# Layer 0's front in another order, with all 16 shifted copies of each channel tile issued from GpSimd

## The chip, the cores and the metric

One core of a Trainium2 chip runs the whole program. TensorE (PE) multiplies, VectorE (DVE), ScalarE (ACT) and GpSimd (POOL) do the rest, and DMA queues move data; SyncE (SP) only issues DMAs. The metric is the device time of one execution in microseconds, lower is better.

## The reference

Two decoder layers run over 512 prompt rows and 8 x 8 sample rows. Only layer 0's mixer matters here:

```
z = rmsnorm(x, norm1[0]) @ conv_w_in                # 1024 -> 2*768 + 256
u = z[:, :768] * sigmoid(z[:, 768:1536])            # GLU
y = causal depthwise conv of u, width 31, 768 channels, + bias
mix = silu(layernorm(y))                            # over the 768 channels
qm = z[:, 1536:]                                    # queries into 256 memory tokens, 4 heads
km, vm = rmsnorm(mem) @ w_mem_kv[0]                 # for the prompt; cached for the samples
x = x + concat(mix, attend(qm, km, vm)) @ w_out     # then a SwiGLU FFN; layer 1 follows
```

## The kernel before

**Weights.** All big products run on an exact split of float32: a chunk of weights is loaded by SP into one of two `raw` buffers, ACT rounds it to `wH` (`hi`, L1111), DVE makes the rest `wL` (`lo`, L446), and PE adds three products (`product`, L1626). SP's loads (`conv_load`, L2255) wait until the buffer's last chunk has been split (`lo_done`). Whatever else SP issues stands in the same queue.

**Front (0 to 46 us).** ACT's queue loads x (`xin`), POOL's loads the memory tokens (`mem`, L2406), and SP's loads the small vectors (`vrow`), the taps `dwrow`, two weight chunks and the conv history (`crow`). PE transposes x and the vectors; it waits for `vec_in`, which counts `dwrow` too. ACT squares x in five pieces (L1272) with `hi(0)` between the second and the third, so that the last three squares wait for the first weight chunk. The row sums go back through PE (L1797) as a broadcast, and `norm(0)` (L466, L1129, L470) makes the activations in eight steps that pace the first product. `lo(1)` follows the norm.

**Taps.** Each of six channel tiles (c = 0 to 5) is convolved by PE and DVE. PE takes `PE_GROUPS[c]` groups of four taps (L1815, L1818): it multiplies `Q`, four copies of `gated` shifted by 0 to 3 columns, with diagonal matrices `diag`. `shifted(c)` makes `Q` by 16 DMAs of 32 partitions (L2276, SP's queue); it waits for `gated` of tile c (`u_done`) and for PE's last use of `Q` (`taps_ready`), since there is one `Q`. `diagonals(c)` (POOL, L2431) needs `dwq`, 16 small DMAs of `dwp` (L2311, SP). DVE adds the taps that are left, 15 of 31 for tiles 0 to 3, none for 4 and 5 (`taps`, L737 and L741).

**Order.** PE's order is written by hand: products 0 and 1 (queries), conv tile 0 (two products), four memory chunks (L1714, the key-value product), conv tile 1, then for c = 2 to 5 conv tile c and `taps(c-1)`, with one prompt unit or sample group of the memory attention between matmul steps. Sample keys (`ks`) are transposed in conv tile 1 (`group_keys`, L1856); POOL loads them with the sample values `vs` when the last memory chunk has been used. At the end PE sums tiles 0 to 3 over channels (`sums`, L1936), runs `taps(5)` with the second sample group between its steps, and sums tiles 4 and 5.

**LayerNorm.** DVE subtracts the mean (L853), ACT squares (L1398) into two buffers of `sq`, DVE adds the six squares one after another (L860), and PE sums the result once. ACT copies `usc` (conv state of the samples, L1392) ahead of the squares. Then come the square root (L1400), DVE's reciprocal (L863), ACT's copies of the new conv states (L1407, L1409), Silu (L1412) and the split of the result, and the output projection at 276 us.

Of the kernel before, what the change touches and what calls it, by code (L numbers as in the profile page):

```python
# [39 lines left out]
def build(nc, x_prompt, x_sample, cache_conv, cache_fox_k, cache_fox_v, cache_fox_logf,  # L40
# [38 lines left out]
    PE_GROUPS = [4] * (KC - 2) + [NQT] * 2  # L79
# [37 lines left out]
    VEC_LOADS, LATE_LOADS = 6 + 8 + 1, 2 + 1  # L117
# [35 lines left out]
    with ExitStack() as ctx:  # L153
# [93 lines left out]
        Q, o = at("Q", [P, 4, UL], o)  # L247
        diag, o = at("diag", [P, 2, 4, NQT, DQ], o)
# [13 lines left out]
        dg = sq[:].rearrange("p a n -> p (a n)")[:, 0:(TT + 1) * P].rearrange("p (t q) -> p t q", q=P)  # L262

# [72 lines left out]
        vec_in, hist_in, mem_in, pages_in = (sem(n) for n in ("vec_in", "hist_in", "mem_in", "pages_in"))  # L336
# [96 lines left out]
        def _(dve):  # L433
# [271 lines left out]
            last.then_inc(dg_done, 1)  # L705

# [143 lines left out]
            squares = tmp[:, 0]  # L850
            for c in range(KC + 1):
                if c < KC:
                    nc.vector.tensor_tensor(yc[:, c], yc[:, c], rb[:], ALU.subtract).then_inc(lny_done, 1)  # L853
                if c == 1:
                    dve.wait_ge(ysq_done, 1)
                    nc.vector.tensor_copy(squares, sq[:, 0]).then_inc(ysq_used, 1)
                elif c:
                    dve.wait_ge(ysq_done, c)
                    dve.wait_ge(ysq_used, c - 1)
                    nc.vector.tensor_tensor(squares, squares, sq[:, (c - 1) % 2], ALU.add).then_inc(ysq_used, 1)  # L860
# [242 lines left out]
        def _(act):  # L1103
# [175 lines left out]
            norm(0)  # L1279
# [60 lines left out]
            hi(1)  # L1340
# [38 lines left out]
            y_begin(KC - 2)  # L1379
            for b in range(GS):  # L1380
                group_keys(1, b)
# [9 lines left out]
            for c in range(KC):  # L1391
                last = nc.scalar.activation(usc[:, c], sample_rows(c)[:, :, NQ:NQ + H], ACT.Copy)  # L1392
            last.then_inc(usc_done, 1)
            for c in range(KC):
                act.wait_ge(lny_done, c + 1)
                if c >= 2:
                    act.wait_ge(ysq_used, c - 1)
                nc.scalar.activation(sq[:, c % 2], yc[:, c], ACT.Square).then_inc(ysq_done, 1)  # L1398
# [192 lines left out]
        def _(pe):  # L1591
# [201 lines left out]
            transposes([dwrow[:, c * P:(c + 1) * P] for c in range(KC)])  # L1793
# [4 lines left out]
            mm.then_inc(ss_ready, 1)  # L1798

# [5 lines left out]
            def taps(c, beside=None):  # L1805

                pe.wait_ge(q_in, 16 * 4 * TAPS * (c + 1))
                pe.wait_ge(diag_ready, c + 1)
                n = PE_GROUPS[c]
                for q in range(n):  # L1810
# [3 lines left out]
                    for a in range(4):  # L1814
                        nc.tensor.matmul(ps[DQ * a:DQ * a + DQ, 4, 0:SEQ], diag[0:k, c % 2, a, q, :], Q[0:k, a, TAPS * q:TAPS * q + SEQ],  # L1815
                                         start=(q == 0), stop=(q == n - 1), skip_group_check=True, tile_position=(0, DQ * a))
                    for a in range(4):
                        mm = nc.tensor.matmul(ps[DQ * a:DQ * a + DQ, 5, 0:NS].rearrange("p (b n) -> p b n", b=NB), diag[0:k, c % 2, a, q, :],  # L1818
                                              Q[0:k, a, H + SEQ:UL].rearrange("p (b n) -> p b n", b=NB)[:, :, TAPS * q:TAPS * q + NQ],
# [114 lines left out]
            def sums(src, c, first, last, bank):  # L1934
                for h in range(2):
                    mm = nc.tensor.matmul(ps[:, bank + h, 0:HT], ones[:], src[:, h * HT:(h + 1) * HT], start=first, stop=last)  # L1936
                if last:
                    mm.then_inc(ln_ready, 1)
            history(0)
            history(1)  # L1940
            product(0, 0, 0, aH, aL, 0, KD, True, True, (a_ready, 0))
            product(1, 0, 1, aH, aL, 0, KD, True, True, beside=lambda k: head_sums(0) if k == 5 else None)
# [24 lines left out]
            for c in range(KC - 2, KC):  # L1967
                pe.wait_ge(y_begun, c + 1)
                sums(yc[:, c], c, False, c == KC - 1, 0)
            group_out(1)  # L1970
            pe.wait_ge(ysq_used, KC)
            sums(tmp[:, 0], 0, True, True, 4)
# [275 lines left out]
        def _(sp):  # L2248
# [20 lines left out]
            def shifted(c):  # L2269

                sp.wait_ge(u_done, c + 1)
                if c:
                    sp.wait_ge(taps_ready, c)
                for g in range(TAPS):
                    for a in range(4):
                        sp.dma_start(Q[DQ * g:DQ * g + DQ, a, 0:UL - g], gated[DQ * a:DQ * a + DQ, c, g:UL]).then_inc(q_in, 16)  # L2276

# [21 lines left out]
            sp.dma_start(dwrow[:], conv_dw[0]).then_inc(vec_in, 16)  # L2299
            assert loads + 1 == VEC_LOADS  # L2300
            conv_load(0)
            conv_load(1)
            for G in range(GR):
# [4 lines left out]
            sp.wait_ge(dwp_done, 1)  # L2308
            for g in range(TAPS):
                for a in range(4):  # L2310
                    sp.dma_start(dwq[DQ * g:DQ * g + DQ, a], dwp[DQ * a:DQ * a + DQ, g]).then_inc(dwq_in, 16)  # L2311
            for n in range(2, C_WO0 + 4):
                if n == C_MEM0 + 3:
                    shifted(0)
                for c in range(1, KC):
                    if n == MP + N_MEM + 2 * (c + 2) + 1:
                        shifted(c)
# [61 lines left out]
        def _(pool):  # L2379
# [28 lines left out]
            def sample_loads(l, G):  # L2408

                mb = MBS[l]  # L2410
                for name, cache, semaphore in (("ks", cache_mem_k, ks_in), ("vs", cache_mem_v, vs_in)):
                    if G and name == "ks":
                        if l:
                            pool.wait_ge(tr_free, marks["ksT", l, G - 1])
                        else:
                            pool.wait_ge(sk_in, GS * G)
                    elif G:
                        pool.wait_ge(at_pv, (2 * len(MEM_UNITS) + GR if l else 0) + G)
                    pool.dma_start(mb[name][:].rearrange("p b t n -> p (b t) n"),
                                   cache[l, G * GS:(G + 1) * GS].rearrange("b (t p) h d -> p (b t) (h d)", p=P)).then_inc(semaphore, 16)  # L2420
# [6 lines left out]
            def diagonals(c):  # L2427

                if c >= 2:
                    pool.wait_ge(taps_ready, c - 1)  # L2430
                nc.gpsimd.tensor_tensor(diag[:, c % 2], dwq[:, :, c, :].unsqueeze(3).broadcast_to([P, 4, NQT, DQ]),  # L2431
                                        m32[:].unsqueeze(1).unsqueeze(1).broadcast_to([P, 4, NQT, DQ]), ALU.mult).then_inc(diag_ready, 1)
            memory(0)
            one = lambda instruction: step(instruction, which=1)
            one(nc.gpsimd.memset(m32[:], 0.0))
            for a in range(4):
                one(nc.gpsimd.affine_select(out=m32[:], in_=m32[:], compare_op=ALU.not_equal, fill=1.0, base=-DQ * a, pattern=[[-1, DQ]],
                                            channel_multiplier=1))
            pool.wait_ge(dwq_in, 16 * 4 * TAPS)
# [73 lines left out]
            sample_loads(1, 0)  # L2513
            sample_loads(1, 1)
# [57 lines left out]
```

## Time and profile before

| | us |
|---|---|
| median of 3 runs | 1941.47 (1938.92 to 1941.77) |
| the profiled execution | 1936.35 |
| its span, first to last instruction | 1934.7 |
| PE busy in the span | 1706.0 (88%) |
| layer 0's mixer in the span, up to the output projection | 276 |
| POOL busy in the span | 114.3 (6%) |

The profiled execution is 5.1 us under the median of the runs; 1.65 us of it lie outside the span. Times in the text are from the span's start. The granted TensorE clock is given in parts of full speed: 1.00 is 2.4 GHz and 0.50 is 1.2 GHz.

### The profile page before, as it was taken

To read this page: it belongs to the slowest core of one execution; us is meant where nothing else is said; L and a number is where in the kernel's file an instruction comes from. 1 tells how busy PE (TensorE), PEld (TensorE's weight loads), DVE (VectorE), ACT (ScalarE), POOL (GpSimd) and SP (SyncE) were. 2 spreads that over 40 slices of the span, in tenths; PEclk is the share of its full clock that TensorE was granted. 3 is DMA by queue.
4 is the path that set the end of the run, shared out by engine and by line. 5 is a ranking of instruction groups with operands and counts; after the bars stand their busy time and mean duration, and the time that the engine had idled before them with its cause. 6 is when DMAs were issued, how large, how long until landed. Compare 5 with 4: busy or idle time off the path is not lost.

```text
span 1934.7 us, 37856 instructions
## 1 busy us (share of the span) xinstructions
PE 1706.0 (88%) x15345; PEld 1494.4 (77%) x15345; DVE 865.3 (45%) x1209; ACT 588.7 (30%) x1050; POOL 114.3 (6%) x220
## 2 busy tenths in 40 slices
PE   4889868999999998999867777788779899999999
PEld 3767567999999997899644444444449899999998
DVE  5657365333323223675466555555414533333121
ACT  4344253322222112433322333333322322222121
POOL 1011000000000001444100000000000000000000
PEclk7899979999999999999886788888869899999999
DMA  4464311222223232233425677777662222223331
GB/s 125 124 176 117 94 51 54 85 79 79 84 87 93 76 89 69 61 81 83 157 93 187 220 253 256 259 258 262 199 205 77 66 82 81 87 82 93 103 88 55
DMA packets 245588, 235.37 MB, mean 122 GB/s; under 512 B 14594, under 2 KB 202644, under 8 KB 245466
## 3 DMA queue, kind: packets, MB, share of 16 engines
q1 hardware_dynamic: 235914, 212.54, 35.7%
q0 software_dynamic: 8896, 18.79, 3.3%
q10 hardware_dynamic: 656, 2.36, 0.3%
q8 instruction: 83, 1.36, 0.3%
q14 instruction: 39, 0.32, 0.1%
HBM read 215.37 MB, written 7.80 MB: 115 GB/s over the span
## 4 chain that ended last, share of the span: by engine, by line
PE 76%; DVE 9%; DMA 5%; SPq 3%; issue 3%; ACT 3%; POOL 0%; DVEq 0%; ACTq 0%; POOLq 0%
PE ps L1626 57%; DMA vring<-in_cache_fox_v_dram 4%; PE ps L2149 4%; PE ps L2194 2%; PE ps L1815 2%; DVE tmp L466 1%; PE ps L2128 1%; SPq L2345 1%; DVE aL L470 1%; PE ps L1605 1%; PE ps L1714 1%; PE ps L1695 1%; DVE yc L737 1%; PE ps L2154 1%; DMA raw<-in_conv_w_in_dram 1%
## 5 line engine op out<-in xcount | busy, mean ns | idle before, releaser
L1626 PE MATMUL ps<-aH,wH 128*128 128x288 f32 x2224 | 490.1, 302 | 41.1 <-DVE aL L470 32.1
L1626 PE MATMUL ps<-aH,wL 128*128 128x288 f32 x2224 | 478.4, 297 | 0.0
L1626 PE MATMUL ps<-aL,wH 128*128 128x288 f32 x2224 | 478.1, 297 | 0.0
L1626 PEld LDWEIGHTS ps<-aH,wH 128*128 128x128 f32 x2224 | 360.5, 191 | 55.2 <-issue 32.4
L446 DVE TENSOR_TENSOR wL<-raw,wH 128x1024 fp32r<-128x1024 f32 (+1 forms) x179 | 232.0, 1296 | 301.8 <-ACT wH L1111 299.4
L1626 PEld LDWEIGHTS ps<-aL,wH 128*128 128x128 f32 x2224 | 361.4, 191 | 0.0
L1626 PEld LDWEIGHTS ps<-aH,wL 128*128 128x128 f32 x2224 | 361.3, 191 | 0.0
L1111 ACT ACTIVATE wH<-raw 128x1024 fp32r<-128x1024 f32 (+1 forms) x179 | 198.8, 1111 | 364.8 <-PE ps L1626 323.2
L1626 PE MATMUL ps<-gH,wH 128*128 128x288 f32 x704 | 151.6, 296 | 0.0
L1626 PE MATMUL ps<-gH,wL 128*128 128x288 f32 x704 | 151.0, 295 | 0.0
L1626 PE MATMUL ps<-gL,wH 128*128 128x288 f32 x704 | 150.9, 295 | 0.0
L2194 PE MATMUL ps<-vring,pTs 128*32 128x256 f32 x768 | 93.2, 485 | 58.7 <-DMA vring<-in_cache_fox_v_dram 57.4
L660 DVE TENSOR_TENSOR tmp<-ps,sq 128x576 f32<-128x576 f32 x44 | 33.3, 758 | 178.3 <-PE ps L1626 178.3
L1626 PEld LDWEIGHTS ps<-gL,wH 128*128 128x128 f32 x704 | 112.8, 188 | 0.0
L1626 PEld LDWEIGHTS ps<-gH,wH 128*128 128x128 f32 x704 | 112.7, 188 | 0.0
L1626 PEld LDWEIGHTS ps<-gH,wL 128*128 128x128 f32 x704 | 112.7, 188 | 0.0
L992 DVE STREAM_TRANSPOSE kset<-kset 128x1536 f32<-128x1536 f32 x64 | 109.5, 1751 | 0.0
L2194 PEld LDWEIGHTS ps<-vring,pTs 128*32 128x32 f32 x768 | 27.2, 125 | 103.2 <-DMA vring<-in_cache_fox_v_dram 80.2
L1250 ACT ACTIVATE gH<-tmp 128x576 f32 (+1 forms) x44 | 30.2, 686 | 246.2 <-DVE tmp L660 246.2
L636 DVE TENSOR_TENSOR xT<-xT,ps 128x576 f32<-128x576 f32 (+1 forms) x32 | 24.1, 754 | 150.5 <-PE ps L1626 150.5
L2149 PE MATMUL ps<-kset,qx 32*32 32x256 f32 x3072 | 76.3, 414 | 4.9 <-issue 4.8
L2149 PEld LDWEIGHTS ps<-kset,qx 32*32 32x32 f32 x3072 | 58.6, 109 | 19.4 <-issue 12.2
(352 smaller groups left out, 1670.3 us busy)
## 6 DMA issues: line engine op xcount, KB each, us to landing
kset<-in_cache_fox_k_dram SPq DMA_DIRECT2D x128, 384.0 KB, 4.0
vring<-in_cache_fox_v_dram SPq DMA_DIRECT2D x128, 384.0 KB, 4.8
raw<-in_w_gate_up_dram SPq DMA_DIRECT2D x88, 512.0 KB, 3.8
raw<-in_w_down_dram SPq DMA_DIRECT2D x32, 704.0 KB, 4.5
raw<-in_fox_w_in_dram SPq DMA_DIRECT2D x21, 512.0 KB, 4.0
raw<-in_w_out_dram SPq DMA_DIRECT2D x16, 512.0 KB, 3.7
raw<-in_conv_w_in_dram SPq DMA_DIRECT2D x14, 512.0 KB, 4.5
raw<-in_w_mem_kv_dram SPq DMA_DIRECT2D x8, 512.0 KB, 3.5
```

Source lines behind the costliest of these rows:

```text
L446: nc.vector.tensor_tensor(wL[s][:, 0:size], raw[:, s, 0:size], wH[s][:, 0:size].bitcast(F32), ALU.subtract).then_inc(lo_done, 1)
L466: nc.vector.scalar_tensor_tensor(out=tmp[:, k % 2], in0=xT[:, k], scalar=vec[:, gain + k:gain + k + 1], in1=rb[:], op0=ALU.mult, op1=ALU.m ...
L470: nc.vector.tensor_tensor(aL[:, k - 1], tmp[:, (k - 1) % 2], aH[:, k - 1].bitcast(F32), ALU.subtract).then_inc(a_ready, 1)
L636: nc.vector.tensor_tensor(x, x, acc(j0 % 2), ALU.add).then_inc(x_new, 1)
L660: nc.vector.tensor_tensor(halves(tmp[:, f0 % 2]), acc(2 * (f0 % 2) + 1), halves(sq[:, f0 % 2]), ALU.mult).then_inc(g_done, 1)
L992: nc.vector.transpose(where, where).then_inc(kt_done, 1)
L1111: nc.scalar.activation(wH[s][:, 0:size], raw[:, s, 0:size], ACT.Copy).then_inc(hi_done, 1)
L1250: nc.scalar.activation(gH[:, f, :].rearrange("p o n -> p (o n)"), tmp[:, f0 % 2], ACT.Copy).then_inc(gH_done, 1)
L1626: mm = nc.tensor.matmul(ps[:, 2 * slot + h, 0:HT], weights[:, w], a[:, k0 + k, h * HT:(h + 1) * HT], start=(first and x == 0 and weights i ...
L1815: nc.tensor.matmul(ps[DQ * a:DQ * a + DQ, 4, 0:SEQ], diag[0:k, c % 2, a, q, :], Q[0:k, a, TAPS * q:TAPS * q + SEQ], start=(q == 0), stop=( ...
L2149: nc.tensor.matmul(out(a, j).rearrange("p (g i) -> p g i", g=SPG), qx4[r, blk, :], kset[x][r, :, blk * DQ:blk * DQ + DQ], start=(m == 0 an ...
L2194: mm = nc.tensor.matmul(ps[QR * j:QR * j + QR, 4, 0:4 * DH], pTs[:, k, QR * j:QR * j + QR], vring[n % VRING][:, 4 * DH * j:4 * DH * (j + 1 ...
```

## The change

- **Front.** `dwrow` gets its own semaphore and is loaded after the two weight chunks. POOL loads `mem` after all of x. ACT runs all squares of x first, then `hi(0)`, `hi(1)`, `norm(0)`, and only then the squares of `mem`. DVE runs `lo(0)`, `lo(1)`, `norm(0)`, and only then the tap rows (`dwp`) and the history. PE transposes `dwrow` after the broadcast of the row sums, and the second half of the history in product 1.
- **Queues.** The 16 DMAs of `dwq` and the 96 of `Q` go from SP's queue to POOL's. `ks` is loaded as soon as `mem` has been read, `vs` at its old place.
- **Last tile.** Tile 5 has its own buffer `Qlast` (over the activations `aH`, which are free by then), so its copies don't wait for `taps(4)`. Tile 4 gets 4 groups on PE and 15 taps on DVE, which stand around the second sample group's softmax steps.
- **LayerNorm.** The squares go to four buffers; PE sums tiles 0 to 3 itself, DVE adds only the last two. `usc` is copied earlier, and a Silu of one column behind the square root brings Silu's table load forward.

```diff
-    PE_GROUPS = [4] * (KC - 2) + [NQT] * 2
+    PE_GROUPS = [4] * (KC - 1) + [NQT]
...
+        Qlast, e_ = at("Qlast", [P, 4, UL], aH_at)
+        def square_of(c):
+            return (sq, tmp)[c // 2 % 2][:, c % 2]
+        def copies(c):
+            return Qlast if c == KC - 1 else Q
...
             lo(0)
+            lo(1)
             norm(0)
-            lo(1)
+            tap_rows()
+            history(0)
+            lo(2)
             memory_rows(0)
-            history(0)
             history(1)
-            lo(2)
...
+            taps(KC - 2, 0)
             group_top(1)
+            taps(KC - 2, 1)
             group_scale(1)
+            taps(KC - 2, 2)
...
-            for c in range(KC + 1):
-                if c < KC:
-                    nc.vector.tensor_tensor(yc[:, c], yc[:, c], rb[:], ALU.subtract).then_inc(lny_done, 1)
...
+            for c in range(KC):
+                nc.vector.tensor_tensor(yc[:, c], yc[:, c], rb[:], ALU.subtract).then_inc(lny_done, 1)
+            dve.wait_ge(ysq_done, KC)
+            nc.vector.tensor_tensor(square_of(KC - 1), square_of(KC - 1), square_of(KC - 2), ALU.add).then_inc(ysq_used, 1)
...
-                if t == 1:
-                    hi(0)
...
+            hi(0)
+            hi(1)
+            norm(0)
             memory_rows(0)
-            norm(0)
...
+            nc.scalar.activation(stat[:, 63:64], eps[:, 0:1], ACT.Silu)
...
+            for c in range(KC - 2):
+                pe.wait_ge(ysq_done, c + 1)
+                sums(square_of(c), c, c == 0, False, 4, ysq_summed)
+            pe.wait_ge(ysq_used, 1)
+            sums(square_of(KC - 1), KC - 1, False, True, 4)
...
+            def shifted(c):
+                pool.wait_ge(u_done, c + 1)
+                if 0 < c < KC - 1:
+                    pool.wait_ge(taps_ready, c)
+                for g in range(0, TAPS):
+                    for a in range(4):
+                        pool.dma_start(copies(c)[DQ * g:DQ * g + DQ, a, 0:UL - g], gated[DQ * a:DQ * a + DQ, c, g:UL])\
+                          .then_inc(q_sw_last if c == KC - 1 else q_sw, 16)
...
+            for t in range(TT + 1):
+                pool.wait_ge(x_in[t], 16)
             memory(0)
...
             diagonals(0)
+            pool.wait_ge(tr_free, marks["memory", 0, KD // 2 - 1])
+            sample_keys(0, 0)
+            shifted(0)
             diagonals(1)
             pool.wait_ge(w_used, C_MEM0 + N_MEM)
-            sample_loads(0, 0)
+            sample_values(0, 0)
             memory_stores(0)
+            shifted(1)
             diagonals(2)
-            sample_loads(0, 1)
-            for c in range(3, KC):
-                diagonals(c)
+            sample_keys(0, 1)
+            sample_values(0, 1)
+            for c in range(2, KC):
+                shifted(c)
+                if c + 1 < KC:
+                    diagonals(c + 1)
```

## Rows read from the trace of the kernel before

**Rows 1.** Windows of two stretches: length, busy time by engine, clock, DMA share, GB/s.
```profile
75.00:102.00 27.00, 14.96 (x49) 11.22 (x50) 12.99 (x19) 6.79 (x8) 3.16 (x4) 0.79 0.73 199
...
170.20:192.30 22.10, 21.27 (x193) 16.73 (x194) 18.70 (x44) 9.92 (x20) 1.91 (x1) 1.00 0.51 127
```

**Rows 2.** Timeline of the front: start, us, engine, line, tiles [idle before <-releaser].
```profile
17.57 0.18 PEld L1605 LDWEIGHTS ps<-ident,vrow 70*128 70x128 f32 x1 [4.75 <-DMA dwrow<-in_conv_dw_dram]
...
19.30 1.06 ACT L1111 ACTIVATE wH<-raw 128x1024 fp32r<-128x1024 f32 x1 [10.82 <-DMA raw<-in_conv_w_in_dram]
...
22.73 1.06 ACT L1272 ACTIVATE tmp<-xin 64x1024 f32<-64x1024 f32 x1
...
30.67 3.20 DVE L466 SCALAR_TENSOR_TENSOR tmp<-xT,vec,rb 128x576 f32<-128x576 f32 x2 [2.40 <-ACT rb L1126]
31.11 4.53 POOL L2431 TENSOR_TENSOR diag<-dwq,m 128x1024 f32<-128x1024 f32 x2 [25.33 <-DMA dwq<-dwp]
...
33.80 2.46 DVE L470 TENSOR_TENSOR aL<-tmp,aH 128x576 fp32r<-128x576 f32 x1
...
36.29 0.82 DVE L466 SCALAR_TENSOR_TENSOR tmp<-xT,vec,rb 128x576 f32<-128x576 f32 x1
...
47.69 0.53 PE L1626 MATMUL ps<-aH,wH 128*128 128x288 f32 x2 [0.35 <-DVE wL L446]
```

**Rows 3.** Timeline of PE, where it had waited, and the start of one tap block.
```profile
82.15 0.79 PE L1714 MATMUL ps<-wH,mH 128*128 128x512 f32 x1 [4.02 <-DVE wL L446]
...
101.75 1.11 PE L1856 MATMUL ps<-ident,ks 128*128 128x128 f32 x4 [5.47 <-DMA ks<-in_cache_mem_k_dram]
...
143.98 1.07 PE L1815 MATMUL ps<-Q,diag 128*32 128x512 f32 x8 [2.65 <-issue]
...
188.13 1.07 PE L1815 MATMUL ps<-Q,diag 128*32 128x512 f32 x8
...
230.08 1.94 PE L1815 MATMUL ps<-Q,diag 128*32 128x512 f32 x8 [6.09 <-issue]
```

**Rows 4.** Windows of two PE stretches, columns as in rows 1.
```profile
82.15:87.50 5.35, 5.35 (x12) 3.79 (x12) 0.00 (x0) 0.00 (x0) 0.00 (x0) 0.51 0.79 216
...
218.16:222.24 4.08, 4.08 (x19) 3.19 (x19) 0.00 (x0) 0.89 (x2) 0.00 (x0) 1.00 0.51 122
```

**Rows 5.** Timeline of SP's queue: one tile's copies.
```profile
170.25 11.17 SPq L2276 DMA_DIRECT2D Q<-gated  x16
```

**Rows 6.** DMA issues: tiles, queue, count, KB each, median us to landing.
```profile
Q<-gated SPq DMA_DIRECT2D x24, 105.8 KB, 2.2
```

**Rows 7.** Timeline of POOL's DMA issues, and DVE beside one of them.
```profile
264.35 1.09 POOL L2401 DMA_DIRECT2D out_dram<-stS  x2
...
777.78 0.49 POOL L2495 DMA_DIRECT2D lfrow<-in_cache_fox_logf_dram  x1 [0.67 <-issue]
...
945.63 0.57 POOL L2401 DMA_DIRECT2D out_dram<-ktok  x1 [15.18 <-DVE ktok L942]
...
945.25 1.21 DVE L446 TENSOR_TENSOR wL<-raw,wH 128x1024 fp32r<-128x1024 f32 x1
```

**Rows 8.** Timeline of DVE, ACT and PE from the last tap to Silu.
```profile
210.65 0.74 DVE L737 SCALAR_TENSOR_TENSOR yc<-gated,dw,yc 128x512 f32<-128x512 f32 x1
...
211.51 0.74 DVE L737 SCALAR_TENSOR_TENSOR yc<-gated,dw,yc 128x512 f32<-128x512 f32 x1
...
213.03 0.21 DVE L721 TENSOR_TENSOR gated<-ps,sq 128x64 f32<-128x64 f32 x1
...
244.46 0.76 DVE L848 TENSOR_SCALAR rb<-ps 128x576 f32<-128x576 f32 x1 [6.73 <-PE ps L1936]
...
246.67 1.86 ACT L1392 ACTIVATE usc<-gated 128x240 f32<-128x240 f32 x6
...
255.87 2.29 PE L1936 MATMUL ps<-tmp,ones 128*128 128x288 f32 x4 [11.23 <-DVE tmp L860]
...
263.51 1.28 ACT L1412 ACT_TABLE_LOAD   x1
```

More of the change, by code:

```diff
@@ L705, in _, with tap_rows @@
             last.then_inc(dg_done, 1)
+            def tap_rows():
+                link(nc.vector.memset(dwp[:], 0.0))
+                bank = group()
+                taps_of = bank[:, 0:KC * W].rearrange("p (c w) -> p c w", c=KC)
+                whole = taps_of[:, :, 0:TAPS * (NQT - 1)].rearrange("p c (q g) -> p g c q", g=TAPS)
+                for g in range(TAPS):
+                    nc.vector.tensor_copy(dwp[:, g, :, 0:NQT - 1], whole[:, g])
+                nc.vector.tensor_copy(dwp[:, 0:TAPS - 1, :, NQT - 1], taps_of[:, :, TAPS * (NQT - 1):W].rearrange("p c g -> p g c")).then_inc(dwp_done, 1)
+                nc.vector.tensor_copy(dw[:], taps_of).then_inc(tr_free, 1)
             def history(n):
@@ L1379, in _ @@
             y_begin(KC - 2)
+            act.wait_ge(u_done, KC)
+            for c in range(KC):
+                last = nc.scalar.activation(usc[:, c], sample_rows(c)[:, :, NQ:NQ + H], ACT.Copy)
+            last.then_inc(usc_done, 1)
             for b in range(GS):
@@ L1391, in _ @@
             for c in range(KC):
-                last = nc.scalar.activation(usc[:, c], sample_rows(c)[:, :, NQ:NQ + H], ACT.Copy)
-            last.then_inc(usc_done, 1)
-            for c in range(KC):
                 act.wait_ge(lny_done, c + 1)
-                if c >= 2:
-                    act.wait_ge(ysq_used, c - 1)
-                nc.scalar.activation(sq[:, c % 2], yc[:, c], ACT.Square).then_inc(ysq_done, 1)
+                if c >= 4:
+                    act.wait_ge(ysq_summed, c - 3)
+                nc.scalar.activation(square_of(c), yc[:, c], ACT.Square).then_inc(ysq_done, 1)
             act.wait_ge(ln_ready, 2)
             nc.scalar.activation(halves(rb[:]), ps[:, 4:6, 0:HT], ACT.Sqrt, bias=eps[:, 2:3], scale=1.0 / CH).then_inc(ln_root, 1)
+            nc.scalar.activation(stat[:, 63:64], eps[:, 0:1], ACT.Silu)
             for n in range(2 * (GR + 1)):
@@ L1792, in _ @@
             transposes([vrow[:]])
-            transposes([dwrow[:, c * P:(c + 1) * P] for c in range(KC)])
             pe.wait_ge(dg_done, 1)
@@ L1798, in _ @@
             mm.then_inc(ss_ready, 1)
+            pe.wait_ge(dw_in, 16)
+            transposes([dwrow[:, c * P:(c + 1) * P] for c in range(KC)])
             def history(n):
@@ L1805, in taps @@
             def taps(c, beside=None):
-                pe.wait_ge(q_in, 16 * 4 * TAPS * (c + 1))
+                last = c == KC - 1
+                pe.wait_ge(q_sw_last if last else q_sw, 16 * 4 * TAPS * (1 if last else c + 1))
                 pe.wait_ge(diag_ready, c + 1)
@@ L1814, in taps @@
                     for a in range(4):
-                        nc.tensor.matmul(ps[DQ * a:DQ * a + DQ, 4, 0:SEQ], diag[0:k, c % 2, a, q, :], Q[0:k, a, TAPS * q:TAPS * q + SEQ],
+                        nc.tensor.matmul(ps[DQ * a:DQ * a + DQ, 4, 0:SEQ], diag[0:k, c % 2, a, q, :], copies(c)[0:k, a, TAPS * q:TAPS * q + SEQ],
                                          start=(q == 0), stop=(q == n - 1), skip_group_check=True, tile_position=(0, DQ * a))
@@ L1932, in conv_tile, with sums @@
                     product(conv_chunk(c) + s, 0, s, aH, aL, 0, KD, True, True, beside=lambda k: beside(c, s, k))
-            def sums(src, c, first, last, bank):
+            def sums(src, c, first, last, bank, taken=None):
                 for h in range(2):
@@ L1938, in sums @@
                     mm.then_inc(ln_ready, 1)
+                elif taken is not None:
+                    mm.then_inc(taken, 1)
             history(0)
-            history(1)
             product(0, 0, 0, aH, aL, 0, KD, True, True, (a_ready, 0))
-            product(1, 0, 1, aH, aL, 0, KD, True, True, beside=lambda k: head_sums(0) if k == 5 else None)
+            product(1, 0, 1, aH, aL, 0, KD, True, True, beside=lambda k: head_sums(0) if k == 5 else history(1) if k == 6 else None)
             memory_rows(0, 0)
@@ L1966, in _ @@
             group_values(1)
-            for c in range(KC - 2, KC):
-                pe.wait_ge(y_begun, c + 1)
-                sums(yc[:, c], c, False, c == KC - 1, 0)
+            pe.wait_ge(y_begun, KC)
+            sums(yc[:, KC - 1], KC - 1, False, False, 0)
+            pe.wait_ge(y_done, KC - 1)
+            sums(yc[:, KC - 2], KC - 2, False, True, 0)
             group_out(1)
-            pe.wait_ge(ysq_used, KC)
-            sums(tmp[:, 0], 0, True, True, 4)
+            for c in range(KC - 2):
[3 more added lines that the diff above has]
+            sums(square_of(KC - 1), KC - 1, False, True, 4)
             pe.wait_ge(oT_hi, GR)
@@ L2267, in ffn_chunks @@
                         load(C_DN[l] + s, columns(w_down[l], P * j, s * KF2, KF2), j)
[L2269 to L2276, printed above, removed]
             def conv_load(n):
@@ L2298, in _ @@
                     loads += 1
-            sp.dma_start(dwrow[:], conv_dw[0]).then_inc(vec_in, 16)
-            assert loads + 1 == VEC_LOADS
+            assert loads == VEC_LOADS
             conv_load(0)
             conv_load(1)
+            sp.dma_start(dwrow[:], conv_dw[0]).then_inc(dw_in, 16)
             for G in range(GR):
@@ L2512, in _ @@
             pool.wait_ge(w_used, C_MEM1 + N_MEM)
-            sample_loads(1, 0)
-            sample_loads(1, 1)
+            for G in range(GR):
+                sample_keys(1, G)
+                sample_values(1, G)
             assert GR == 2
```

66 lines of the change are left out of this document (24 added, 42 removed).

## The prediction

> **What bounds the kernel now.** I read the page first: PE is busy in 88% of the span, so time is to be had only where PE waits or does work that can go elsewhere. Windows by stage then show where that is. The conv tiles are bound by PE: 21.27 of 22.10 us busy at full clock. The stretch from 75 to 102 us is not, with 14.96 of 27.00 us at a mean clock of 0.79 [rows 1]. The timeline names the waits. In the front the norm starts only at 30.67 us, behind the squares of x (the last starts at 22.73), which stand behind the first weight chunk (19.30). POOL's first `diag`, 31.11 to 35.64, runs into the norm: two DVE steps take 3.20 us where one alone takes 0.82, and the third takes 2.46 [rows 2]. Later PE waits 4.02 us for a split chunk, 5.47 for `ks`, 2.65 and 6.09 us for copies of `Q` [rows 3]. Last, from 244.46 to 255.87 us PE waits for DVE's chain of added squares [rows 8].
>
> **The front.** Today the norm starts 7.94 us after the last square (30.67 - 22.73) [rows 2]. In the new order no square waits for weights: they follow x, which PE has transposed before 17.57 us, where it stands waiting for `dwrow` [rows 2]. The squares and the broadcast then end near 18 us, and what is late next is the second weight chunk, since `hi(1)` stands before ACT's part of the norm and `lo(1)` before DVE's. The first chunk lands by 19.30 [rows 2]; without 1 MB of `mem` and without `dwrow` ahead of it I put the second at 19 us, an estimate. ACT's split (1.06) and DVE's (1.2) follow, so the norm starts at about 21.5 us: 9.2 us sooner. `diag` leaves the norm: 3.20 + 2.46 - 3 x 0.82 is 3.2 us. Sum: -12.5. Bounds: if the second chunk lands three us later, -9.5; if it lands with the first and PE's 0.35 us at 47.69 goes too, -15. The tap rows, `dwq` and `diag(0)` now come after the norm; PE wants them only in `taps(0)`, some 50 us later, so that cover is wide. SP's loads stand behind nothing but `lo_done` from then on.
>
> **Memory chunks.** The 4.02 us for `lo` of the third chunk stay: DVE's order ahead of it is the old one. That chunk runs at half clock, 12 matmuls in 5.35 us [rows 4]. The fourth waits today for a load that stands behind the 16 copies on SP; conv tile 1 starts some 94.7 us (101.75 - 5.47 - two steps of 0.8) [rows 3]. With the load on time, the fourth follows at 87.5 and takes 2.7 us at full clock or 5.35 at half: 1.9 to 4.5 us. I take -4, since work without a gap brings the clock back.
>
> **Sample keys.** `ks` may be loaded once `mem` is read, some 35 us before PE wants it, and POOL has only `dwq` and `diag(0)` ahead of it. PE's 5.47 us go [rows 3], and the slow clock after it (four transposes in 1.11 us) brings up to 1 more: -6, bounds -5.5 to -7. `vs` now follows `shifted(0)` and `diag(1)` but still waits for the last memory chunk, as today; its use is some 20 us later.
>
> **The copies.** On SP one tile's 16 took 11.17 us with their waits [rows 5] and 2.2 us to land [rows 6]. On POOL this program has no copy of 32 partitions. The nearest rows: two stores of 120 partitions in 1.09 us, one of 128 in 0.57 beside a two-input DVE operation that took its usual 1.21 us; and, far off, one-row loads with a register load between them, 0.67 + 0.49 = 1.16 us each [rows 7]. Bounds 0.49 and 1.16 us; I take 0.55, nearest in kind. 16 x 0.55 + 2.5 is 11.3 us. The window is 17.9 us (170.25, when the copies may start, to 188.13, when the next taps do) [rows 3, 5], so the copies are hidden up to 0.96 us each; POOL's `diag` behind them is wanted a whole tile later. Here SP's queue loses its 10 us blocks, and the late copies of tile 1 (2.65 us) [rows 3], which shared their time with `ks` and `vs` loads now queued behind them: -2.65, bounds 0 and -2.65.
>
> POOL's `diag` beside two-input operations of DVE slowed both: 4.53 us for two where one alone takes 1.91, and 3.20 for two norm steps [rows 1, 2]. [...]
>
> **Tail.** Today `taps(5)` starts at 230.08 us: `Q` is free when `taps(4)` ends, then come 16 copies. With `Qlast` they start when `gated` of tile 5 is done, 213.24 [rows 8], and land at 224.5: -5.6. PE has `taps(4)` (half as long), the first sums and the sample keys to do meanwhile, to about 220. But DVE now has 15 taps of tile 4, 0.86 us each (211.51 - 210.65) [rows 8]. Five are done early; then DVE stands in `group_top` until PE has made the scores inside `taps(5)`, and the other ten (8.6 us) follow, with the scaling between. Five of them (4.3 us) now lie between the scores and the probabilities, where PE has three tap groups of about 1 us, so PE waits some 2.5 us; and the mean needs tile 4, some 0.3 us more. Today the mean comes 14.4 us after `taps(5)` starts (244.46 - 230.08) [rows 3, 8]; now 17.2: -5.6 + 2.8 = -2.8. Bounds +4 (copies at 1 us each) and -6 (no wait).
>
> **LayerNorm.** From the mean (244.46) to the sum of squares PE starts at 255.87 and ends 2.29 us later [rows 8]: 13.7 us. ACT squares from 248.5, behind the `usc` copies (246.67 + 1.86) [rows 8]; without them it starts 2.2 us after the mean, and PE sums each tile while the next is squared: 4.08 us for four at full clock [rows 4]. DVE's one addition hides under these. 2.2 + 0.7 for the first square, 4.1 and 1.0 make 8 us: -5.6. At half clock each sum takes 2.29 us and the gain is nothing: bounds 0 and -6. Before it PE idles some 2.5 us; it came out of 2.65 us at full speed (1.07 us per eight matmuls at 143.98) and out of 6.09 at half (1.94) [rows 3], so I take full clock. The Silu table load (1.28 us) [rows 8] only moves ahead of the conv-state copies, which Silu waits for anyway: nothing, ±0.5.
>
> **Sum.** -12.5 - 4 - 6 - 2.65 - 2.8 - 5.6 = -33.5 us, nearly all of it waiting. After the output projection starts, PE works through in the same order, nothing there is tied to absolute time, and the shift carries to the end. The profiled execution, 1936.35, becomes 1902.8. It lies 5.1 us under the median of the runs, 1941.47, which becomes 1908; I say 1907.
>
> **Rivals.**
> - *Part of it stays* (chance 0.20). The second weight chunk lands late (-9.5 instead of -12.5) and the sums of squares run at half clock (0 instead of -5.6): -25 us, 1916. For it: the clock is at 0.51 after a wait of 4 us [rows 3, 4]. Against: the shorter wait.
> - *The copies go at the pace of the one-row loads* (0.10). Beyond 0.96 us each copy costs its excess 16 times in four tiles, and in the tail every excess over 0.55 counts 16 times: with c us each, 4(16c - 15.4) + 16(c - 0.55) = 80c - 70.4. At 1.16: 22 us back, -11, 1930. Against: the register load between those is not part of a copy.
> - *POOL is locked out by DVE's taps and the kernel is slower* (0.07). If each copy waits for one whole tap, 0.55 + 0.86 = 1.41 us: 42 us back, +9, 1950. It decides from 1.30 us (80c - 70.4 = 33.5). For it: `diag` beside the norm. Against: that is arithmetic on whole rows, while the store beside DVE lost nothing [rows 7].
> - *No change* (0.03): the gaps in front of `ks` and the norm come back through a wait that I don't see, as at the 4.02 us that DVE's own queue sets [rows 3].
>
> **How the numbers follow.** Full forecast 0.60. Its own range is 1899 to 1914: the bounds of the front and the tail, most of them independent. The second and third case reach to 1930; leaving out half of the second rival's upper part and the third gives 1897 to 1924 for 8 in 10. A measurement of this kernel tells 0.2% (4 us) from no change. Faster: 0.60 + 0.20 + 0.10 = 0.90; same 0.03; slower 0.07.
>
> **What would show it.** Right: norm from about 21 us with steps of 0.82; no gap before the fourth memory chunk and before `ks`; copies on POOL at about 0.55 us; tap blocks that follow the conv products without a gap; `taps(5)` from about 12 us after `gated` of tile 5; PE's sums of squares between ACT's squares. Wrong: copies at 1 us and more, then gaps ahead of each tap block; a norm that still waits for weights at 25 us; PE at 0.50 through the sums; DVE's taps of tile 4 ending long after `taps(5)`.

## The result and the profile after

| | us |
|---|---|
| median before, run beside the kernel after | 1941.62 (1938.92 to 1943.14) |
| median after | 1919.20 (1915.14 to 1922.88) |
| ratio | 0.9886, 95% interval 0.9861 to 0.9910 |
| the profiled execution after, its span | 1921.13, 1919.5 |

The kernel became 22 us faster. That lies inside the 1897 to 1924 us given for 8 cases in 10, but outside the full forecast's own 1899 to 1914, and it is two thirds of the 33.5 us forecast. The profiles show where. I use the start of DVE's reciprocal in the LayerNorm as a mark for the whole front. Before, it stands here (timeline of DVE):

```profile
258.96 3.75 DVE L863 RECIPROCAL rb<-rb 128x576 f32<-128x576 f32 x1 [1.81 <-ACT rb L1400]
```

The next fence is the timeline of the kernel after, in the order of time within each of its three parts: front, one conv tile, tail.

```profile
18.35 1.55 DVE L477 SCALAR_TENSOR_TENSOR tmp<-xT,vec,rb 128x576 f32<-128x576 f32 x2 [0.34 <-ACT rb L1136]
22.25 0.84 PE L1616 MATMUL ps<-ident,dwrow 31*128 31x31 f32 x6 [4.68 <-DMA dwrow<-in_conv_dw_dram]
25.02 1.06 PE L1616 MATMUL ps<-ident,crow 120*128 120x120 f32 x4 [1.92 <-DMA crow<-in_cache_conv_dram]
25.74 0.83 PE L1637 MATMUL ps<-aH,wH 128*128 128x288 f32 x2
68.97 0.79 PE L1725 MATMUL ps<-wH,mH 128*128 128x512 f32 x1 [4.08 <-DVE wL L457]
...
99.76 7.88 POOL L2431 DMA_DIRECT2D Q<-gated  x16 [14.81 <-PE ps L1831]
105.80 0.28 DVE L754 SCALAR_TENSOR_TENSOR yc<-gated,dw,yc 128x64 f32<-128x64 f32 x1
106.66 3.02 DVE L754 SCALAR_TENSOR_TENSOR yc<-gated,dw,yc 128x64 f32<-128x64 f32 x1
107.66 1.93 POOL L2443 TENSOR_TENSOR diag<-dwq,m 128x1024 f32<-128x1024 f32 x1
109.61 0.74 DVE L750 SCALAR_TENSOR_TENSOR yc<-gated,dw,yc 128x512 f32<-128x512 f32 x1
112.18 0.94 PE L1850 MATMUL ps<-ident,prob 128*128 128x128 f32 x4 [3.58 <-DVE prob L774]
112.77 0.83 PE L1637 MATMUL ps<-aH,wH 128*128 128x288 f32 x2
...
211.95 1.93 PE L1828 MATMUL ps<-Qlast,diag 128*32 128x512 f32 x8 [2.72 <-issue]
222.62 0.44 PE L1885 MATMUL ps<-ident,prob 128*128 128x128 f32 x2 [2.39 <-DVE prob L796]
228.40 0.76 DVE L865 TENSOR_SCALAR rb<-ps 128x576 f32<-128x576 f32 x1 [1.54 <-PE ps L1949]
231.33 3.70 PE L1949 MATMUL ps<-sq,ones 128*128 128x288 f32 x8 [2.75 <-ACT sq L1408]
238.95 3.75 DVE L873 RECIPROCAL rb<-rb 128x576 f32<-128x576 f32 x1 [1.01 <-ACT rb L1410]
```

**Front.** The norm starts 12.3 us earlier than in [rows 2], and `ks` no longer keeps PE waiting as it did in [rows 3].

**Conv tile.** The 16 copies leave POOL in 7.88 us, 0.49 each, and beside them a tap takes 0.28 us as ever. Then `diag` starts, right behind the copies, and the tap beside it takes 3.02 us in place of 0.28. The taps stand ahead of the scaling of the probabilities, so PE waits 3.58 us, and the matmuls behind it take 0.83 us for two, where [rows 2] has 0.53 at full clock. The same comes in four tiles: the stretched tap takes 3.02, 2.62, 2.58 and 2.58 us, PE's wait is 3.58, 3.17, 3.13 and 3.14. Windows over two tiles of the kernel after (columns as in rows 1) show its price: 24.43 and 27.06 us for a period that was 22.10 in [rows 1], the first at full clock, the second at a mean clock of 0.87.

```profile
121.91:146.34 24.43, 21.26 (x194) 16.70 (x193) 19.65 (x40) 9.91 (x19) 9.81 (x17) 1.00 0.41 102
...
172.26:199.32 27.06, 23.92 (x193) 19.38 (x192) 21.91 (x45) 9.91 (x19) 9.80 (x17) 0.87 0.37 104
```

The DMA issues of the kernel after put the landing of copies on POOL's queue at 3.4 to 4.7 us, against 2.2 on SP's [rows 6]; PE's taps in tiles 1 to 4 follow their products without a gap all the same.

```profile
Q<-gated POOLq DMA_DIRECT2D x20, 105.8 KB, 3.4
...
Q<-gated POOLq DMA_DIRECT2D x20, 105.4 KB, 4.7
```

### The profile page after: what moved, and what is told of

The parts are those of the page before. It is cut to its first block, busy times and chain, and to the rows that moved or that the text cites. A ratio compares the mean times of both kernels' runs of the same rounds, so it can differ in the third digit from the quotient of the medians.

```text
span 1919.5 us, 37784 instructions
## 1 busy us (share of the span) xinstructions
PE 1714.4 (89%) x15297; PEld 1504.2 (78%) x15297; DVE 883.4 (46%) x1234; ACT 588.8 (31%) x1051; POOL 169.8 (9%) x332
## 3 DMA queue, kind: packets, MB, share of 16 engines
q10 hardware_dynamic: 656, 2.36, 0.4%
## 4 chain that ended last, share of the span: by engine, by line
PE 77%; DVE 9%; DMA 5%; SPq 3%; issue 3%; ACT 3%; POOL 0%; DVEq 0%; POOLq 0%; ACTq 0%
PE ps L1637 58%; PE ps L2167 4%; DMA vring<-in_cache_fox_v_dram 4%; PE ps L2212 2%; PE ps L2146 1%; PE ps L1828 1%; SPq L2345 1%; DVE tmp L477 1%; PE ps L1616 1%; DVE yc L750 1%; DVE rb L487 1%; DVE yc L754 1%; PE ps L2128 1%; DMA crow<-in_cache_conv_dram 1%; PE ps L1706 1%
## 5 line engine op out<-in xcount | busy, mean ns | idle before, releaser
L2212 PEld LDWEIGHTS ps<-vring,pTs 128*32 128x32 f32 x768 | 26.7, 124 | 101.5 <-DMA vring<-in_cache_fox_v_dram 80.0
L2167 PE MATMUL ps<-kset,qx 32*32 32x256 f32 x3072 | 81.2, 429 | 9.7 <-issue 9.4
L2401 POOL DMA_DIRECT2D out_dram<-ystage x14 | 9.2, 664 | 882.3 <-ACT ystage L1247 882.3
```

The costliest lines, as they stand in the source:

```text
L2167: nc.tensor.matmul(out(a, j).rearrange("p (g i) -> p g i", g=SPG), qx4[r, blk, :], kset[x][r, :, blk * DQ:blk * DQ + DQ], start=(m == 0 an ...
L2212: mm = nc.tensor.matmul(ps[QR * j:QR * j + QR, 4, 0:4 * DH], pTs[:, k, QR * j:QR * j + QR], vring[n % VRING][:, 4 * DH * j:4 * DH * (j + 1 ...
```

## The experiments

All are edits of the kernel after. Medians are of 5 or 6 runs each, beside runs of the kernel before on the same chip, whose medians there were 1944.1 (experiments 1, 4, 5 and 7), 1943.9 (8 to 11) and 1944.8 us (2, 3 and 6). The kernel after was not run again beside them; where a median is compared with its own, that goes by the ratio to the kernel before, 0.9886 (0.9861 to 0.9910). Behind the mark the profiles of all thirteen kernels take 1674 to 1684 us (span minus mark), and most of the difference arises in layer 1, which no edit touches. So a term of a few us is read from the mark, and the median decides only where it moves by more. Marks, spans and medians do not move alike: from before to after the mark moves by 20.0 us, the span by 15.2 and the median by 22.4; from before to experiment 1 it is 33.4, 32.5 and 41.5. The profile before is of an execution faster than the medians of its kernel.

**1. `diag` ahead of the copies.**

```diff
-            shifted(1)
             diagonals(2)
+            shifted(1)
...
             for c in range(2, KC):
-                shifted(c)
                 if c + 1 < KC:
                     diagonals(c + 1)
+                shifted(c)
```

> The copies stay on POOL; only `diagonals(c+1)` moves ahead of `shifted(c)` in POOL's order, for c from 1 to 4. Theory A: the four tiles lose their time because `diag`, now behind the copies, falls into DVE's chain of two-input taps. Then every small tap takes 0.28 us again, `diag` runs as the taps of PE end, the period of a conv tile goes from 23.8-27.1 us back to about 22.1 us, and the kernel takes about 13 us less than the changed one: 1906 us. Rival B: it is the 16 DMA issues of POOL (7.9 us per tile) beside DVE's taps, or the granted clock, that cost the time; then the order of `diag` changes nothing: 1919 us, within 3. Rival C: `diag` first delays the copies by 1.9 us and the next taps wait for them: gaps of 1 to 2 us ahead of the tap blocks, and 1912 us.

Measured: 1902.62 us (1898.15 to 1904.30), ratio to before 0.9775 (0.9748 to 0.9801). One window and the timeline of this kernel:

```profile
116.68:138.77 22.09, 21.26 (x194) 16.72 (x193) 19.14 (x45) 9.91 (x19) 10.04 (x17) 1.00 0.53 139
```

```profile
120.89 2.17 POOL L2443 TENSOR_TENSOR diag<-dwq,m 128x1024 f32<-128x1024 f32 x1 [10.47 <-PE ps L1831]
123.00 7.92 POOL L2431 DMA_DIRECT2D Q<-gated  x16
125.46 0.74 DVE L750 SCALAR_TENSOR_TENSOR yc<-gated,dw,yc 128x512 f32<-128x512 f32 x1
126.12 0.28 DVE L754 SCALAR_TENSOR_TENSOR yc<-gated,dw,yc 128x64 f32<-128x64 f32 x1
130.61 0.66 PE L1850 MATMUL ps<-ident,prob 128*128 128x128 f32 x4 [0.83 <-DVE prob L774]
...
196.87 1.52 PE L1828 MATMUL ps<-Qlast,diag 128*32 128x512 f32 x8 [4.02 <-issue]
207.83 0.69 PE L1885 MATMUL ps<-ident,prob 128*128 128x128 f32 x2 [2.38 <-DVE prob L796]
218.04 3.78 PE L1949 MATMUL ps<-sq,ones 128*128 128x288 f32 x8 [2.75 <-ACT sq L1408]
225.53 3.75 DVE L873 RECIPROCAL rb<-rb 128x576 f32<-128x576 f32 x1 [0.81 <-ACT rb L1410]
```

Theory A holds: `diag` runs while DVE has no taps, all 75 small taps take 0.28 us, PE's wait is back at 0.83, the period at 22.09, and the mark comes 13.4 us earlier (238.95 - 225.53). The copies, all still on POOL and 2 us later, cost DVE nothing, so B falls; no tap block of tiles 1 to 4 waits, so C falls.

**2 and 3. `diag` inside the copies**, behind 4 (`after` is 1) or behind 8 of them (`after` is 2).

```diff
-            def shifted(c):
+            def shifted(c, after=None):
...
                 for g in range(0, TAPS):
+                    if g == after:
+                        diagonals(c + 1)
                     for a in range(4):
...
```

> `diag(c+1)` stands inside the copies, behind the first 4 of 16. It then runs from about 2 us after the taps of PE end, beside DVE's maximum of the scores (one operand) and before DVE's first tap, which comes 5 us after them. Theory A (it is two-input operations of DVE that `diag` collides with): nothing is lost, small taps 0.28 us, as with `diag` first, 1903 us. Rival: any place behind copies is bad, whatever DVE does just then: 1910 or more.

> `diag(c+1)` stands behind 8 of the 16 copies, so it runs from about 4.0 to 5.9 us after the taps of PE end, and DVE's first tap wants to start at 5.0. Theory A: a partial collision; DVE loses 0.8 to 2 us per tile in place of 2.3 to 2.7, PE's wait for the probabilities grows from 0.83 to 1.6 to 2.8 us, and the kernel takes 3 to 9 us more than with `diag` first: 1906 to 1912. Rival: DVE's tap goes first and `diag` waits for it, so that nothing is lost: 1903.

Measured: behind 4 copies 1902.81 us (1899.78 to 1904.07), ratio 0.9783 (0.9762 to 0.9803); behind 8 copies 1915.14 (1910.48 to 1920.48), 0.9851 (0.9826 to 0.9877). Timeline of the kernel with 4, then of that with 8:

```profile
123.63 0.69 DVE L765 TENSOR_REDUCE stat<-ps 128x2 f32<-128x512 f32 x1 [1.95 <-PE ps L1843]
123.82 1.92 POOL L2445 TENSOR_TENSOR diag<-dwq,m 128x1024 f32<-128x1024 f32 x1
125.86 0.74 DVE L750 SCALAR_TENSOR_TENSOR yc<-gated,dw,yc 128x512 f32<-128x512 f32 x1
```

```profile
128.57 1.93 POOL L2445 TENSOR_TENSOR diag<-dwq,m 128x1024 f32<-128x1024 f32 x1
128.64 2.42 DVE L750 SCALAR_TENSOR_TENSOR yc<-gated,dw,yc 128x512 f32<-128x512 f32 x1
135.47 0.66 PE L1850 MATMUL ps<-ident,prob 128*128 128x128 f32 x4 [2.50 <-DVE prob L774]
```

Two us of POOL's order decide: the mark is at 227.08 with 4 copies and at 233.66 with 8. Beside the maximum (L765, one operand, 0.69 us with `diag` and without) nothing is lost. Beside the first tap, that tap ends only after `diag`, 2.42 us for 0.74; in the four tiles it takes 1.96, 2.42, 2.33 and 2.33. PE's wait is 2.50 us, inside the 1.6 to 2.8 expected, the period of tiles 2 to 4 is 23.7 us, and the mark comes 8.1 us after that of experiment 1, as theory A has it. The median of 1915.14 lies above the 1906 to 1912 expected; of the 4.4 us that it moves more than the mark, 3.2 lie behind the mark in the two profiles.

**4. Copies on SP's queue again.**

```diff
             for n in range(2, C_WO0 + 4):
+                if n == C_MEM0 + 3:
+                    shifted(0)
+                for c in range(1, KC):
+                    if n == MP + N_MEM + 2 * (c + 2) + 1:
+                        shifted(c)
                 conv_load(n)
...
-            shifted(0)
             diagonals(1)
...
-            shifted(1)
             diagonals(2)
...
```

> All copies go through SP's queue again, at the places they had before the change; everything else of the changed kernel stays (front, sample keys, `Qlast`, tail, LayerNorm), and POOL makes `diag` as soon as the taps before it are done. Theory A (`diag` collides with DVE's taps): no collision, so about as fast as with `diag` first, plus up to 2.65 us for the late copies of tile 1 and the start of SP's copies of tile 5 behind its loads: 1907 to 1910 us. Rival B (POOL's DMA issues slow DVE or PE): as fast, 1906 to 1909, while `diag` first with copies on POOL stays at 1919. Rival D (neither; the time is lost by what the new order does to PE's clock): 1919 in both.

Measured: 1914.83 us (1909.42 to 1921.07), ratio 0.9839 (0.9809 to 0.9870); the mark is at 236.79. SP's queue, then PE, in this kernel's timeline:

```profile
102.09 11.12 SPq L2294 DMA_DIRECT2D Q<-gated  x16
123.99 1.94 PE L1828 MATMUL ps<-Q,diag 128*32 128x512 f32 x8 [3.49 <-issue]
206.62 1.94 PE L1828 MATMUL ps<-Qlast,diag 128*32 128x512 f32 x8 [5.00 <-issue]
```

No collision, as A and B expected, and yet 11.3 us behind experiment 1 at the mark, far more than the 2.65 us I had allowed: PE waits 3.17 us for the fourth memory chunk, whose load stands behind SP's copies, then 3.49 us for the copies of tile 1 (the 2.65 us of [rows 3] again), and 5.00 in place of 4.02 us for tile 5's. These make 7.6 us; much of the rest is PE's slower steps behind them (1.94 us for eight tap matmuls behind the 3.49 us, where experiment 1 has 1.07). The median lies above both expected ranges and below D's 1919. So POOL's queue is the better place here; only `diag` stood wrong in it.

**5. PE makes all taps of tile 4**, on the kernel after.

```diff
-    PE_GROUPS = [4] * (KC - 1) + [NQT]
+    PE_GROUPS = [4] * (KC - 2) + [NQT] * 2
...
-            pe.wait_ge(y_done, KC - 1)
```

> PE makes all taps of tile 4 again (8 groups in place of 4), so DVE has no taps between the last conv product and the mean; the rest of the changed kernel stays. The prediction held that DVE's ten late taps put about 2.5 us ahead of the probabilities and 0.3 us ahead of the mean, and that PE had room for the other four groups before the copies of tile 5 land. By this, PE's wait of 2.39 us for the probabilities and the wait ahead of the mean go, PE works 4.3 us more in `taps(4)`, and `taps(5)` starts at about the same time if that work fits before the copies land: -2 to 0 us, 1917 to 1919. Rival: `taps(4)` with 8 groups pushes `taps(5)` back by its full 4.3 us, so 1921 to 1924.

Measured: 1913.60 us (1908.34 to 1917.52), ratio 0.9829 (0.9802 to 0.9856), below the 1917 to 1919 expected. The collisions still blur it: from the issue of tile 5's copies to the mark it takes 34.8 us in place of 37.7, while tiles 1 to 4 came out 2.4 us slower (103.9 us from the issue of tile 1's copies to that of tile 5's, for 101.5).

**6. The same with `diag` first.**

> Two moves only: `diag` of tiles 2 to 5 ahead of the copies (alone 1902.6 us) and all 8 tap groups of tile 4 on PE. Theory: DVE's taps of tile 4 cost the tail 6 to 7 us (with the three other moves, the two kernels with and without them stand 8.4 us apart at the LayerNorm's end), and the transposes inside product 0 give back nothing that lasts, since PE then waits for DVE's `stage`: 1895 to 1897 us, as fast as with all moves. Rival: the transposes and the early `diag` carry part of it: 1898 to 1900.

Measured: 1899.27 us (1894.72 to 1900.93), ratio 0.9762 (0.9741 to 0.9784). Its timeline:

```profile
197.61 1.06 PE L1828 MATMUL ps<-Qlast,diag 128*32 128x512 f32 x8 [0.75 <-issue]
210.21 0.76 DVE L865 TENSOR_SCALAR rb<-ps 128x576 f32<-128x576 f32 x1 [6.86 <-PE ps L1949]
213.14 2.21 PE L1949 MATMUL ps<-sq,ones 128*128 128x288 f32 x8 [2.75 <-ACT sq L1408]
219.07 3.75 DVE L873 RECIPROCAL rb<-rb 128x576 f32<-128x576 f32 x1 [0.81 <-ACT rb L1410]
```

PE's four more groups fill the wait for the copies (0.75 us left of 4.02), the wait for the probabilities is gone, and PE stays at full clock, so its sums of squares take 2.21 us for eight in place of 3.78. The mark is 6.5 us earlier than in experiment 1, as the theory has it, so by the mark the change's own edit of `PE_GROUPS` costs 6.5 us. The median moves by 3.4 us only, into the rival's range, and the two ratios are not told apart; experiments 8 and 9, which differ by the same edit, give 8.4 us at the mark and 11.2 in the median.

**7. The transposes of `dwrow` and `crow` inside product 0**, ahead of its last two steps.

> PE's transposes of `dwrow` and of the first `crow` half move from ahead of product 0 to inside it, ahead of its seventh and eighth step. Theory: product 0 waits only for these two loads (PE stands 4.68 and 1.92 us for them, and starts at 25.74 us although the first operands are ready at 20.7), and runs behind the norm otherwise; the last `aL` is done at 30.66, so product 1 starts at about 32 us in place of 34.4, and the kernel takes 2 to 3 us less: 1916.5. Rival: PE is at half clock until product 0 has run 5 us without a gap; started early it waits for the norm at every step, stays at half clock into product 1, and nothing is won: 1919 us, product 1 at 34 to 35.

Measured: 1917.72 us (1911.92 to 1923.29), ratio 0.9856 (0.9825 to 0.9886), not told apart from the kernel after. Product 0 starts 4.5 us earlier (21.20 for 25.74) and product 1 at 32.36, as the theory had it, with the clock up by then. But later PE waits 1.11 us for DVE's `stage`, and the first tap block comes only 1.6 us earlier (93.44 for 95.06). So most of PE's two waits in the front seems to be hidden by DVE's chain behind the norm; the collisions, worse in this profile (106.7 us for the four periods from `taps(0)` on, 104.3 in the kernel after), took the rest, and the mark is at 241.81.

**8 and 9. Three moves, and all four.** Experiments 1 and 7 with `diag(1)` straight behind `diag(0)`; then with experiment 5 added.

> Three moves together: `diag` of tiles 2 to 5 ahead of the copies (alone 1902.6 us), PE's transposes of `dwrow` and `crow` inside product 0, and `diag` of tile 1 right behind that of tile 0, so that it no longer stands beside DVE's `lo` of the memory chunks (4.08 us for two where one takes 1.23). Theory: the transposes bring the 1.6 us seen at the first tap block, now not buried by the collisions, and the early `diag` 0 to 1.5 us: 1900 us. Rival: the early `diag`, at 44 us, falls beside DVE's two-input steps for `mem` instead, and the memory products wait 1 to 2 us longer: 1902 to 1903.

> As the combination of three moves, and PE makes all 8 tap groups of tile 4 (DVE none of them). With `diag` first, PE stands 4.02 us ahead of `taps(5)` for the copies of tile 5 (issued 186.27 to 194.11, read from 196.87) and 2.38 us for the probabilities behind DVE's taps. Theory: the four more groups (4 us) fit into the first wait and the second goes: 2.4 to 4 us less than the combination, 1896 to 1898 us. Rival: PE's work ahead grows as much as the wait shrinks and the probabilities come no sooner, since they are bound by DVE's and ACT's own steps: as the combination, 1900.

Measured: three moves 1906.27 us (1903.32 to 1910.08), ratio 0.9799 (0.9775 to 0.9822), mark at 226.45: no gain over experiment 1 (225.53), whose norm started 0.9 us sooner than here. The time is above the theory's 1900 and the rival's 1902 to 1903. The early `diag(1)` takes DVE's two `lo` steps from 4.08 to 2.36 us, yet PE waits the same 4.08 us ahead of the third memory chunk: that collision, which the kernel after has too, does not set PE's wait. All four: 1895.08 us (1894.31 to 1899.15), ratio 0.9752 (0.9727 to 0.9778), mark at 218.01. Between these two the marks lie 8.4 us apart, 0.8 of them the norm's start, more than the 2.4 to 4 expected. It is the fastest kernel here, but not told apart from experiment 6, which has two of the four moves.

**10. DVE's chain of squares again**, with `diag` first.

> `diag` first as in the 1902.6 us kernel, but the squares of the LayerNorm are added by DVE one tile after the other again, and PE sums only the total (with `usc` still ahead). Theory: PE summing each tile is worth what the two traces showed from the mean to the last sum, 13.7 us before and 9.75 us after, less about 1 us for `usc` moved ahead: +3 to +4 us, 1906. Rival: the prediction's lower bound, that PE's sums at half clock give the gain back: 1902.6, within 1.

Measured: 1913.58 us (1911.63 to 1920.39), ratio 0.9841 (0.9816 to 0.9866). PE's one sum waits for DVE again (timeline of this kernel):

```profile
225.81 2.29 PE L1956 MATMUL ps<-tmp,ones 128*128 128x288 f32 x4 [9.46 <-DVE tmp L877]
```

From the mean to the mark it takes 12.7 us (216.17 to 228.90) against 10.4 in experiment 1: 2.3 us, less than the 3 to 4 expected. The median is 11 us above experiment 1's; 7.6 us of that arise behind the mark, in work that the edit doesn't touch, and stay unexplained.

**11. The first sample keys at their old place**, with `diag` first.

> `diag` first as in the 1902.6 us kernel, but the first sample keys are loaded again only when the last memory chunk has been used, together with the values. Theory: PE's 5.47 us wait for `ks` comes back, and with it up to 1 us at the slower clock: +5.5 to +6.5 us, 1908 to 1909. Rival: ahead of the keys stand other waits of about that length (4.08 us for `lo` in the memory chunks), and the load, alone with the weights now, lands sooner: +2 to +3 us, 1905.

Measured: 1913.41 us (1910.47 to 1915.18), ratio 0.9835 (0.9810 to 0.9860). POOL and PE in its timeline:

```profile
76.96 0.96 POOL L2414 DMA_DIRECT2D ks<-in_cache_mem_k_dram  x1 [6.71 <-PE ps L1725]
85.47 1.12 PE L1869 MATMUL ps<-ident,ks 128*128 128x128 f32 x4 [6.18 <-DMA ks<-in_cache_mem_k_dram]
```

The wait is back, 6.18 us, the transposes behind it take 1.12 us for four, and the mark is 9.3 us later (234.84). The theory's sign holds, its price was too low: from conv tile 1 to `taps(0)` it takes 26.11 us in place of 17.35, 6.2 of it this wait and 2.6 PE busy for longer, at a mean clock of 0.87 in place of 1.00, where up to 1 was expected.

## Why the prediction was right or wrong

Steps of the forecast against the marks: start of an operation in us, and in brackets what the step up to it gained against before.

| start of | before | after | `diag` first | forecast |
|---|---|---|---|---|
| norm | 30.67 | 18.35 | 18.70 | |
| first memory product | 71.94 | 58.72 (-13.2) | 58.09 (-13.9) | -12.5 |
| conv tile 1 | 94.54 | 77.66 (-3.7) | 76.82 (-3.9) | -4 |
| `taps(0)` | 118.76 | 95.06 (-6.8) | 94.17 (-6.9) | -6 |
| `taps(1)` | 143.98 | 121.91 (+1.6) | 116.68 (-2.7) | -2.65 |
| mean | 244.46 | 228.40 (+6.0) | 215.10 (-2.1) | -2.8 |
| reciprocal (the mark) | 258.96 | 238.95 (-4.0) | 225.53 (-4.1) | -5.6 |
| sum | | -20.0 | -33.4 | -33.5 |

That the sum of `diag` first meets the forecast is in part luck: up to `taps(0)` it gained 2.1 us more than forecast, and in the tail and the LayerNorm together 2.3 us less.

**The step that failed** is half a sentence under "The copies": "POOL's `diag` behind them is wanted a whole tile later", costed at nothing. I asked who waits for `diag`, not what it would stand beside. Before, it ran as PE's taps ended, with DVE free of taps until 4.6 us later (timeline of the kernel before):

```profile
148.18 1.91 POOL L2431 TENSOR_TENSOR diag<-dwq,m 128x1024 f32<-128x1024 f32 x1 [21.09 <-PE ps L1818]
150.52 0.69 DVE L752 TENSOR_REDUCE stat<-ps 128x2 f32<-128x512 f32 x1 [2.83 <-PE ps L1830]
152.75 0.74 DVE L737 SCALAR_TENSOR_TENSOR yc<-gated,dw,yc 128x512 f32<-128x512 f32 x1
```

The change puts 7.9 us of issues ahead of it and so moves it into the tap chain. The operation, its length and its effect on two-input DVE work were all in [rows 1, 2]: I took 3.2 us out of the front for it and did not look for where it lands next. Experiments 1 to 3 show the cause by moving `diag` alone: 13.4 us at the mark. The four periods from `taps(0)` to `taps(4)` take 104.3 us in the kernel after and 88.8 in experiment 1. Of these 15.5 us, 9.7 are DVE's own loss (10.8 us for four taps of 0.28), and 5.8 are PE busy for longer, at a lower clock in three of the four periods. Experiment 1's front is 0.9 us sooner besides; 3.0 us come back in the tail of the kernel after, 1.3 of them because PE's wait for tile 5's copies is 2.72 us there in place of 4.02.

**Right.** The steps of the norm, undisturbed (1.55 us for two); the memory chunk; `ks`, which experiment 11 shows from the other side; the copies, at 0.49 us on the lower bound. Beside DVE's taps they lose nothing and cost it nothing, which settles the second and the third rival. The Trainium skill's page "SBUF — State Buffer", section "Who interferes with whom", has a DVE instruction with two SBUF inputs contend with a GpSimd instruction that reads SBUF, and a reduction never on this chip. Experiments 2 and 3 agree, with 0.69 us for the reduction and 1.96 to 2.42 for the tap; the reduction here reads PE's results in `ps`, in PSUM, so of reductions over SBUF they show nothing.

**Mis-sized.** The tail: +2.8 us for DVE's taps of tile 4. The wait for the probabilities came as forecast (2.39 for 2.5). In experiment 1 `taps(5)` gains 5.9 us (5.6 forecast) and the mean comes 18.2 us behind it, not 17.2. By my own numbers PE idled from 220 to 224.5 us in this stretch; I did not see that the four groups taken from it fitted there. Experiment 6 puts the edit at 4.9 us up to the mean and 1.6 more through the clock. The LayerNorm: -4.1 for -5.6, since PE's sums start at half clock after those waits. I had taken full clock from the length of the one wait ahead of them, but the same 2.75 us leads to 3.78 us for the first eight matmuls in experiment 1 and to 2.21 in experiment 6; at full clock, in experiment 6, it takes 8.9 us from mean to mark against 14.5 before, the 5.6 us forecast. Front: -13.2 for -12.5, by two misses that largely offset each other. The norm starts 12.3 us sooner, not 9.2, since neither weight chunk is late: ACT splits both without a wait, in 2.12 us from 13.74. But product 0 starts only 10.7 us sooner (36.40 and 25.74), since PE waits for `dwrow` and `crow`, whose transposes stand ahead of it in PE's order; the change loads `dwrow` behind the weights, and the forecast put no price on that.

```profile
36.40 0.82 PE L1626 MATMUL ps<-aH,wH 128*128 128x288 f32 x2 [5.12 <-DVE aL L470]
```

The line is from the timeline of the kernel before; the waits of the kernel after stand in the result.

**The first rival** ("part of it stays", 1916) comes near the time measured, but by another way: the second chunk was not late, and its half-clock sums make up 1.5 us of its 5.6.

## What to carry to other kernels

When work is put ahead of an instruction on its queue, look at what that instruction will run beside at its new time, not only at who waits for its result. In this kernel an arithmetic GpSimd operation over SBUF had its place where DVE had no two-input work, and the DMA issues did not mind, so the operation goes first and the issues behind it. And an edit with several parts is worth taking apart even where it wins: here two of the parts lost 20 of the 40 us that the rest was worth (marks at 258.96, 238.95 and, in experiment 6, 219.07).

## What the runs showed of the hardware

- A 1.92 us `diag` on POOL holds up the tap of DVE that it meets: 0.28 us becomes 2.58 to 3.02 (kernel after), 0.74 becomes 1.96 to 2.42 (experiment 3), while `diag` takes no longer than the 1.91 us of [rows 1]. Beside the norm it did (4.53 us for two, [rows 2]). The held-up tap is recorded from up to 1.0 us before `diag` (106.66 and 107.66), so the timeline alone doesn't say which came first.
- Copies of 32 partitions cost 0.49 us each on POOL and 0.63 to 0.70 on SP (10.06 to 11.12 us for 16 in experiment 4, waits included); they land after 2.6 to 4.7 us (medians, in the profiles after and of experiment 1) and 2.2 us [rows 6].
- A wait of PE of 3.1 to 3.6 us in a period of 22 us cost more than itself in three of the four tiles of the kernel after, where the mean clock was 0.94, 0.93 and 0.87: in the window from 172.26 PE is busy 2.7 us longer than in that from 121.91, with 193 and 194 matmuls. In the one from 121.91, with a wait of 3.17 us, the clock stayed at 1.00 and only the wait was lost, so the length of the wait alone did not decide.
